# Where the fills, the gating and the key splits stand in the last pair of heads of an attention kernel

## What is computed

```python
def latent_attend(q_lat, q_rope, c, kr, w_uv, mask):
    s = (jnp.einsum('bqhk,bsk->bhqs', q_lat, c)
         + jnp.einsum('bqhr,bsr->bhqs', q_rope, kr)).astype(jnp.float32) * ATTN_SCALE
    if mask is not None:
        s = jnp.where(mask, s, NEG_INF)
    p = jax.nn.softmax(s, axis=-1).astype(c.dtype)
    o_lat = jnp.einsum('bhqs,bsk->bqhk', p, c)
    return jnp.einsum('bqhk,khv->bqhv', o_lat, w_uv)
...
    out = jnp.einsum('bte,ed->btd', o * jax.nn.silu(gate), p['w_out_b'][j])
```

## Time and profile before

| | us |
|---|---|
| median of 3 runs | 1962.93 |
| lowest, highest | 1961.89, 1963.22 |
| the profiled execution, its own time | 1963.68 |
| its span in the profile | 1961.8 |

### The profile page before, as it was taken

How to read it: one execution, slowest core, us unless ns; L and a number is a source line. 1 busy time by engine, 2 the same in 40 slices (tenths; PEclk the granted TensorE clock), 3 DMA queues, 4 the chain that set the end, 5 groups by cost and what they waited for, 6 DMA issues and landing times.

```text
span 1961.8 us, 31461 instructions
## 1 busy us (share of the span) xinstructions
PE 1919.9 (98%) x11755; PEld 1813.8 (92%) x11755; DVE 1062.5 (54%) x1942; ACT 768.9 (39%) x1344; POOL 394.5 (20%) x322
## 2 busy tenths in 40 slices
PE   8999999999999999999999999999999989999998
PEld 8999999999988999999989999999999879988886
DVE  4354456445658512422466666676666567653632
ACT  4332333233422222211455555565555467751100
POOL 0221222122311020000043333432432410000000
PEclk9999999999999999999999999999999999999999
DMA  5121122022236312233201121112011343263421
GB/s 171 44 78 46 43 67 78 26 62 68 85 116 197 122 43 73 77 105 120 75 29 49 43 60 51 39 48 66 31 53 42 91 106 97 67 247 134 156 86 43
DMA packets 186066, 158.54 MB, mean 81 GB/s; under 512 B 36128, under 2 KB 170528, under 8 KB 185728
## 3 DMA queue, kind: packets, MB, share of 16 engines
q1 hardware_dynamic: 180912, 139.67, 23.6%
q10 hardware_dynamic: 4896, 17.30, 2.5%
q0 software_dynamic: 176, 0.43, 0.1%
HBM read 115.52 MB, written 41.84 MB: 80 GB/s over the span
## 4 chain that ended last, share of the span: by engine, by line
PE 54%; DVE 7%; issue 5%; ACT 3%; DMA 1%; DVEq 0%; POOL 0%; ACTq 0%; SPq 0%; POOLq 0%
PE ps L115 16%; PE ps L117 16%; PE ps L116 16%; PE ps L1895 2%; PE ps L1878 1%; PE ps L1877 1%; DVE h_pt_l L109 1%; ACT h_p L2011 1%; ACT h_p L2000 1%; DVE h_mx L2137 1%; DVE h_p L2099 1%; DVE h_p L2094 1%; DVE s_mx L2738 1%; PE ps L2405 1%; DMA m_g_raw<-scratch_o 0%
## 5 line engine op out<-in xcount | busy, mean ns | idle before, releaser
L1791 POOL TENSOR_SCALAR h_p<-h_p,h_rsum 128x128 f32<-128x128 f32 (+7 forms) x128 | 220.9, 1728 | 443.0 <-DVE h_rsum L2141 443.0
L115 PE MATMUL ps<-act_h,a_w_l 128*128 128x384 f32 x768 | 271.3, 353 | 0.7 <-DVE act_l L109 0.7
L117 PE MATMUL ps<-act_h,a_w_h 128*128 128x384 f32 x768 | 260.4, 339 | 0.0
L116 PE MATMUL ps<-act_l,a_w_h 128*128 128x384 f32 x768 | 260.2, 339 | 0.0
L115 PE MATMUL ps<-act_h,m_c_l 128*128 128x384 f32 x480 | 162.9, 339 | 0.0
L117 PE MATMUL ps<-act_h,m_c_h 128*128 128x384 f32 x480 | 162.6, 339 | 0.0
L116 PE MATMUL ps<-act_l,m_c_h 128*128 128x384 f32 x480 | 162.5, 339 | 0.0
L115 PEld LDWEIGHTS ps<-act_h,a_w_l 128*128 128x128 f32 x768 | 144.6, 188 | 5.6 <-issue 3.3
L116 PEld LDWEIGHTS ps<-act_l,a_w_h 128*128 128x128 f32 x768 | 144.8, 189 | 3.3 <-issue 3.3
L117 PEld LDWEIGHTS ps<-act_h,a_w_h 128*128 128x128 f32 x768 | 144.4, 188 | 0.0
L104 ACT ACTIVATE h_pt_h<-ps 128x128 fp32r<-128x128 f32 (+2 forms) x192 | 87.1, 490 | 112.0 <-PE ps L1895 111.8
(11 more groups left out here) (319 smaller groups left out, 4827.7 us busy)
## 6 DMA issues: line engine op xcount, KB each, us to landing
a_w_raw<-in_w_in_a SPq DMA_DIRECT2D x32, 512.0 KB, 4.1
m_c_raw<-in_w_in_b SPq DMA_DIRECT2D x20, 512.0 KB, 4.2
scratch_gate<-m_sg SPq DMA_DIRECT2D x16, 576.0 KB, 5.2
o_w_raw<-in_w_out_b SPq DMA_DIRECT2D x16, 512.0 KB, 6.5
h_gate<-scratch_gate SPq DMA_DIRECT2D x62, 128.0 KB, 2.0
scratch_og<-h_gate SPq DMA_DIRECT2D x62, 128.0 KB, 1.7
o_g_raw<-scratch_og SPq DMA_DIRECT2D x24, 256.0 KB, 4.3
a_xn<-in_x SPq DMA_DIRECT2D x9, 512.0 KB, 4.2
```

The source lines that it names most:

```text
L115: nc.tensor.matmul(out, ll, rh, start=first, stop=False)
L116: nc.tensor.matmul(out, lh, rl, start=False, stop=False)
L117: return nc.tensor.matmul(out, lh, rh, start=False, stop=last)
L1791: nc.gpsimd.tensor_scalar(weights_of(u), weights_of(u), rsum[:, u % PB], None, ALU.mult).then_inc(S["p_ready"], 1)
```

## The change

Three moves, all in the last pair. No instruction is added or taken away.

1. POOL's fills of the padding rows (`zero_loads`, after the scaling of u = 6) wait for `proj_out` at one less than its last count: for the projection QB2 in place of QL.
2. On DVE, `first_keys_low(u - 9)` moves from the head of the unit to behind `inverted`, `largest(u + 3)` and `gated`.
3. On DVE in u = 15, `gated(6)` moves from in front of `turned(15)` to behind it.

```diff
@@ -1791,7 +1791,7 @@
                 if last and u == 6:
 
-                    pool.wait_ge(S["proj_out"], PAIRS * NP)
+                    pool.wait_ge(S["proj_out"], PAIRS * NP - 1)
                     k.samples.zero_loads(pool)
@@ -2191,22 +2191,23 @@
                         proj(pr + n, s, first and not n)
-                if last and KEYS_FROM <= u < KEYS_FROM + NKT - 1:
-                    k.samples.first_keys_low(dve, u - KEYS_FROM)
                 if (u % 2 or u == 0) and u + 2 < UNITS:
                     inverted(pr, u + 2)
                 if u + 3 < UNITS:
                     largest(pr, u + 3)
                 if u >= 4 and u % 4 < 2:
                     gated(pr, u // 4 * 2 - 2 + u % 2, last)
+                if last and KEYS_FROM <= u < KEYS_FROM + NKT - 1:
+                    k.samples.first_keys_low(dve, u - KEYS_FROM)
...
-                if u == UNITS - 1:
-                    if not last:
-                        sines(pr + 1, 0)
+                if u == UNITS - 1 and not last:
+                    sines(pr + 1, 0)
                     gated(pr, NG - 2, last)
                 turned(pr, u)
+                if u == UNITS - 1 and last:
+                    gated(pr, NG - 2, last)
```

## The result

| | before | changed |
|---|---|---|
| median of 22 runs, us | 1962.94 | 1967.0 |
| lowest, highest | 1959.54, 1965.45 | 1964.37, 1969.01 |
| the profiled execution, its own time | 1963.68 | 1966.38 |
| its span | 1961.8 | 1964.3 |

A forecast was written before the change was run, and what follows sets the result against it. PE's waits, 5.56 us, were taken as all that reordering could win, with the cache load next. Split stalls of 5.7 less 0.24, 0.75, 1.1 and 0.2 gave 3.4, plus 1.0 for the clock: 4.4, so 1967.3 us, range 1964.2 to 1969.8.

The forecast's parts named there:

- The fills: Before the first key turn: PE comes 3.3 us earlier, then waits for the cache load; 0.2 of 3.5 us kept.
- The 0.2: At the first key turn: the gain kept from the earlier fills, 0.2 us, bounds nothing to 0.5.
- The key splits: Turns of key pieces 1 to 4: PE waits for late splits, 0.75, 1.93, 1.86 and 1.15 us, sum 5.7.
- The stall behind piece 3: At piece 3's turn: late turn 2 delays ACT's exponential, then DVE's reciprocal and maximum; 1.86 us.
- What comes back: From key turn 4 to the values of group 7: time regained, -0.24, -0.75 and -1.1 us.
- the last term: From values of group 6 to group 7: splits are ahead, only the gating is waited for; -1.1 us.
- The clock: Behind the 3.15 us wait at the first key turn: a clock fall costs 1.0 us, bounds 0 and 3.0.
- The 2.25 us wait: PE idle from 970.23 to 972.48 without a clock fall, cited for the 3.4 us case without one.
- Not slower: Rival at the first key turn: the load isn't what PE meets; +0.3 us, about 1963.2, chance 0.10.
- Faster by harmless splits: Rival in DVE's order: the splits bring no stalls; 3.8 us gained at most, 1959.1, chance 0.04.
- No fall of the clock at 3.4 us: Rival: the stalls as worked out but no clock fall behind the load wait; 1966.3 us, chance 0.30.
- The signs: Trace marks of being right: load wait of some 3 us, four key turns waiting, `values(7)` 3 to 5 us later.

The follow-up runs named there:

- e1: The kernel before with only POOL's fills waiting for QB2 in place of QL: 1964.54 us against 1962.98.
- e8: The kernel before with POOL's fills waiting for QB2 and the first cache load issued early on SP: 1959.6 us against 1962.72.
- e9: The changed kernel, no edit, executed once more for its trace alone: 41.99 us from the values of group 1 to those of group 7.
- e2: The kernel before with only the key splits moved behind maximum and gating on DVE: 1966.25 us against 1962.98.
- e10: The changed kernel, no edit, executed a third time for its trace alone: 44.03 us from the values of group 1 to those of group 7.
- e7: The kernel before with the key split moved behind the row maximum in unit 10 alone: 1963.7 us against 1962.72.
- e3: The kernel before with only the gating of group 6 moved behind the last splits on DVE: 1961.0 us against 1962.98.
- e6: The changed kernel, all three moves, with the first cache load issued early on SP: 1963.36 us against 1962.72 for the kernel before.

## Why the prediction was right, point by point

**The fills.** The mechanism was right. The step said that of 3.5 us only 0.2 are kept, since the load stands where it was. PE's wait there was 3.15 by the forecast and 3.40 in the trace, and e1 and e8 show the cover from both sides. The 0.2 itself did not come: the first key turn was 0.21 us later against the pair's start, where 0.2 earlier was forecast. The reason is the landing, and the bounds on it, from nothing to 0.5 us earlier, were too narrow. The time from the values of group 1 to the first key turn, which the landing sets in every kernel that waits for the load, was 13.44 (e1), 13.60 (e9), 14.23 (e2), 14.37 (e10) and 14.51 us (changed), and 14.88 in e7: 1.4 us of scatter, which one trace can't show. In all six the load of 16 KB was issued 7.6 us after those values began. The 1024 KB landed 5.5 to 5.8 us after their issue, the 16 KB 5.7 to 7.2 us after theirs. So it is the small load, which the prediction took for the load as a whole, that scatters and that PE waits for.

**The key splits.** Right in kind and size: 5.7 us forecast by key turn 4, 5.59 measured, no single piece off by more than 0.14. The forecast waits of 0.75, 1.9, 1.9 and 1.4 us read 0.57, 1.76, 1.50 and 1.40 in the trace, since I had given the difference of starts for the first three: without a wait a row's duration reaches some 0.2 us into the next row, and only what goes beyond that shows as idle. The starts are the measure, not the idle time. The stall behind piece 3, where the late turn held up ACT's exponential and this came back to DVE, was the step most open to doubt, and it came (2.04 us of DVE idle for `h_p`).

**What comes back.** Right: -0.45, -0.66 and -1.10 against -0.24, -0.75 and -1.1. The distance from key turn 4 to the turns of unit 15 was 5.68, not 5.89. The step took that ACT's exponential of unit 15 hangs on turn 4's high part alone. Before, it also waited for the row maximum, done at 1572.37, and began 1.35 us after the turn; in the changed kernel the maximum is done earlier and it began 1.19 us after. e3 shows the last term by itself.

**The clock.** This step is the least settled. I took 1.0 us, with 0 to 3.0 as bounds. The profiled execution had no fall in the last pair, so its pair is longer by 3.59 us without one. The medians differ by 4.1, which leaves some 0.5 us, less than the scatter of the landing. In e10 the fall came and cost 1.25 us; in two of three traces of the changed kernel none came there. One in three at 1.25 us would be some 0.4 us, an estimate from three traces. So 1.0 was probably too much, and that it and the 0.2 of the fills missed in opposite directions (0.5 too much, 0.4 too little) is luck that brought the sum within 0.3 us of what was measured. The 2.25 us wait that the prediction counts for the case without a fall is no such sign: in e7's trace the same wait, in code that no kernel here changes, has one. Its stretch behind the wait:

```profile
972.52:975.60 3.08, 3.08 (x14) 3.08 (x15) 2.41 (x5) 2.18 (x6) 0.00 (x0) 0.50 0.88 266
```

That fall cost nothing, since PE then waited for DVE in both: its next wait ended 3.79 us after this stretch's start in e7 and 3.80 in before. The Trainium skill's page "TensorE: Matmul & The Clock Gate", Part 1, says that the unit which judges how busy the array is runs freely and isn't reset when a kernel starts. These traces agree: the wait at the same place of the same kernel had a fall once and twice not.

**The rivals.** Not slower, with the load out of PE's way, was priced at +0.3 and is what e6 is: 1963.36 against 1962.72. Faster by harmless splits is out by e2. No fall of the clock at 3.4 us gives 1966.3, and what was measured, 1967.0, lies between this rival and the forecast.

**The signs.** The waits came as listed. The signs in absolute times are blurred, since the changed kernel's profiled execution came to the pair 0.76 us earlier: the first key turn was at 1556.58, 0.55 us before its old time where 0.3 was allowed, and `values(7)` 2.8 us after its old time where 3 to 5 was given. Against the pair's start they are +0.21 and +3.59. The wait for POOL in front of unit 15's turns was 0.67 us, with 0.35 more in front of key turn 5.

## What to carry to other kernels

Before a wait is taken away, find out what the waiting engine meets next and when that is ready: here the next thing was a load whose issue nothing in the change moved, and the gain of 3.3 us went into it until the load was moved too (1959.6 with it, no gain in the median without). Look also at what the wait counts: here it counts a small load that the waiting turn doesn't read. A step that frees a single buffer for the busiest engine belongs in front of anything that waits for that same engine's latest work; put behind it, the two wait for each other in turn, here at 0.7 to 2.0 us a piece. And a part of a change may be good while the sum is bad: moves 1 and 3 with the early load gave 1958.3, all three without it 1967.0.

## What the runs showed of the hardware that I had not expected

Filler work in a wait cost nothing that the times show and went with a higher mean clock: 0.9967 and 0.9968 with it, 0.9960 and 0.9959 without. A load of 16 KB, issued right behind one of 1024 KB at the same place in the program, landed 5.7 to 7.2 us after its issue in six executions, the 1024 KB 5.5 to 5.8 after theirs; with the early issue both took 5.6 or 5.7. A fall of the clock costs nothing where the engine's next wait takes it up (e7 at 972 us) and next to nothing where it comes early to what it needs next anyway (0.2 us at most in before at 1552). And a wait of 3.40 us had no fall of the clock behind it, while one of 1.98 us had the earlier trace rows (and had not in e2): the length of a single idle stretch does not tell by itself whether the clock falls.
